# Half the tokens by fetched rows, attention and key selection in one stage, value sums kept in PSUM, and GpSimd making every second low part of the expert tiles

## The reference

```python
def memory_cross_attention(h, m, w_xq, w_xkv, w_xo):
    q = (h @ w_xq).reshape(b, s, XA_HEADS, XA_HEAD_DIM)          # 4 heads of 256
    sc = einsum('bshd,bmhd->bhsm', q, k) / sqrt(XA_HEAD_DIM)
    o = einsum('bhsm,bmhd->bshd', softmax(sc), v).reshape(b, s, D_MODEL)
    return o @ w_xo

def peer_ffn(h, w_pq, sub_keys, u_emb, v_emb):                   # 8 heads, 2 x 128 keys, 16384 experts
    q = (h @ w_pq).reshape(b, s, PEER_HEADS, 2, PEER_HALF)
    sc = einsum('bshpc,pnc->bshpn', q, sub_keys)
    top_v, top_i = top_k(sc, 16)
    cand = top_v[..., 0, :, None] + top_v[..., 1, None, :]
    best_v, best_i = top_k(cand, 16)                             # 16 experts of a token and head
    expert = i1 * 128 + i2 ; gate = softmax(best_v)
    a = einsum('bthkd,btd->bthk', u_emb[expert], h)
    return einsum('bthk,bthkd->btd', gelu(a) * gate, v_emb[expert])
```

## Time and profile before

| | us |
|---|---|
| median of 3 runs | 4000.87 (3989.51 to 4028.2) |
| the profiled execution | 3974.28 |
| its span | 3972.5 |
| first head of the selection on DVE starts | about 1712 |
| gate steps | about 2700 to 2944 |
| value groups and tail | about 2944 to 3972.5 |

### The profile page before, as it was taken

One profiled execution on the slowest core, in us unless ns is written; L12 is line 12 of the kernel. 1 busy time (PEld: TensorE's weight loads), 2 busy tenths in 40 slices (PEclk: granted clock), 3 DMA queues, 4 the chain that ended last, 5 costly groups with the idle time before them and its releaser, 6 DMA issues. The chain is left out here.

```text
span 3972.5 us, 61578 instructions
## 1 busy us (share of the span) xinstructions
PE 3687.8 (93%) x21687; PEld 3261.5 (82%) x21687; DVE 3061.8 (77%) x5229; ACT 1455.4 (37%) x2548; POOL 1648.2 (41%) x1269
## 2 busy tenths in 40 slices
PE   6999999999899999988998989998996999999996
PEld 5766676676577886778888989998996999999996
DVE  5676776777753503459999998978976999999998
ACT  3456555565652424222222222224541222222222
POOL 2433444333312120105655455552224556566552
PEclk9999999999899999999999999999998999999998
DMA  2111111111253311138888887895779999999995
GB/s 86 49 48 54 44 47 44 48 54 54 96 191 128 132 53 76 59 123 300 325 327 316 293 325 281 327 357 215 265 266 318 369 382 390 379 374 375 386 392 196
DMA packets 315022, 848.43 MB, mean 214 GB/s; under 512 B 27184, under 2 KB 122672, under 8 KB 310832
## 3 DMA queue, kind: packets, MB, share of 16 engines
q1 hardware_dynamic: 201328, 400.91, 29.4%
q0 software_dynamic: 110592, 402.70, 26.7%
q10 hardware_dynamic: 2880, 41.94, 2.7%
HBM read 726.96 MB, written 118.49 MB: 213 GB/s over the span
## 5 line engine op out<-in xcount | busy, mean ns | idle before, releaser
L1920 POOL DMA_INDIRECT join_urow<-in_u_rows,select_row_now x384 | 510.6, 1330 | 508.3 <-DVE join_rows L2221 223.0
L2672 POOL DMA_INDIRECT spread_vrow<-in_v_rows,spread_row_of x384 | 540.1, 1407 | 409.4 <-DVE spread_y L2740 301.8
L163 PE MATMUL spread_banks<-spread_ahi,spread_vhi 128*128 128x384 f32 (+1 forms) x2048 | 640.7, 313 | 55.7 <-DVE spread_acc L2730 40.3
L163 PE MATMUL select_products<-h_hi,shared_pair_hi 128*128 128x256 f32 (+2 forms) x1856 | 608.4, 328 | 71.5 <-DVE shared_raw_low L1736 66.3
L164 PE MATMUL spread_banks<-spread_alo,spread_vhi 128*128 128x384 f32 (+1 forms) x2048 | 638.2, 312 | 0.0
L165 PE MATMUL spread_banks<-spread_ahi,spread_vlo 128*128 128x384 f32 (+1 forms) x2048 | 638.0, 312 | 0.0
L164 PE MATMUL select_products<-h_lo,shared_pair_hi 128*128 128x256 f32 (+2 forms) x1856 | 603.2, 325 | 0.0
L165 PE MATMUL select_products<-h_hi,shared_raw_low 128*128 128x256 f32 (+2 forms) x1856 | 602.4, 325 | 0.0
L163 PE MATMUL shared_carry<-shared_wide_hi,shared_w_hi 128*128 128x512 f32 x1408 | 558.0, 396 | 27.7 <-DVE shared_wide_lo L591 11.2
L164 PE MATMUL shared_carry<-shared_wide_lo,shared_w_hi 128*128 128x512 f32 x1408 | 553.4, 393 | 0.0
L165 PE MATMUL shared_carry<-shared_wide_hi,shared_w_lo 128*128 128x512 f32 x1408 | 553.0, 393 | 0.0
(11 more groups left out here) (307 smaller groups left out, 6664.0 us busy)
## 6 DMA issues: line engine op xcount, KB each, us to landing
spread_vraw<-in_peer_v SPq DMA_DIRECT2D x124, 512.0 KB, 8.7
shared_raw<-in_select_pairs SPq DMA_DIRECT2D x112, 512.0 KB, 6.5
gates<-spread_stage ACTq DMA_DIRECT2D x20, 2048.0 KB, 7.3
spread_act<-gelu_u SPq DMA_DIRECT2D x128, 320.0 KB, 7.5
spread_graw<-gates SPq DMA_DIRECT2D x32, 1280.0 KB, 11.8
gelu_u<-front SPq DMA_DIRECT2D x100, 320.0 KB, 6.9
shared_w_raw<-in_w_mix SPq DMA_DIRECT2D x56, 512.0 KB, 3.6
shared_w_raw<-in_w_cross SPq DMA_DIRECT2D x32, 512.0 KB, 3.5
```

Of the source, the lines that this page charges most:

```text
L163: nc.tensor.matmul(out, whi, xhi, start=(first and i == 0), stop=False)
L1920: nc.gpsimd.indirect_dma_start(picks.slots[s][:], None, u_rows, bass.IndirectOffsetOnAxis(row_now[:, t, j:j + 1], 0)).then_inc(row_loaded[ ...
L2672: nc.gpsimd.indirect_dma_start(v_slots[s][:], None, v_rows, bass.IndirectOffsetOnAxis(row_of[:, par, t, j:j + 1], 0)).then_inc(row_loaded[ ...
```

## The change

`GT` is 4: 512 tokens, the first half, are fetched ones and the second half is dense (`PICKED` and `DENSE`). Cross attention and selection become one phase, `retrieve_phase`, with one list of tiles (`tile_order`) whose products pass through four PSUM banks in turn (`bank_order`, `Banks`), and four buffers for tiles in their raw, high and low form (`WeightTiles`). The first half's attention goes first and the second half's query projection is laid between its units. Selection runs in 16 blocks: 8 heads of the fetched half, then 8 of the dense half, each over 4 token tiles; each query tile is loaded for both halves. The 128 tiles of `peer_u` lie in blocks 2 to 15, each one product of 512 columns. The second half's output projection, residual and norm lie in blocks 0 and 1. The 512 dots are spread over blocks 1 to 15, with 7 buffers. The expert numbers are found with 16-bit integers, subtract and minimum, in place of a multiplication.

Which engine makes a low part is `maker`: GpSimd for the attention's `ask` and `give` tiles and for odd expert tiles, DVE for the rest. GpSimd's program has the lows among its fetches, in one queue:

```diff
+GT = 4
+TD = ND * P
...
+        self.maker = [int(tile[0] in ("ask", "give") or tile[0] == "expert" and tile[2] % 2) for tile in self.order]
...
+    def load(self, sync, n, src):
+        job = self.order[n - 4]
+        sync.wait_ge(self.banks.filled(job), self.banks.turn(job))
+        sync.dma_start(self.raw[n % 4], src).then_inc(self.loaded[n % 4], 16)
...
+    def split_low(self, eng, of, n):
+        eng.wait_ge(self.high_made, n + 1)
+        of.tensor_tensor(self.low[n % 4], self.raw[n % 4], self.high[n % 4].bitcast(F32), ALU.subtract
+                         ).then_inc(self.low_made[self.maker[n]], 1)
...
+    tiles += query(0) + query(1) + [("give", 1, k) for k in range(NC)] + query(2)
+    for b in range(FIRST_DENSE, BLOCKS):
+        for i, e in enumerate(experts_of(b)):
+            tiles.append(("expert", 1, e))
+            if i == QUERY_BEHIND and b + 1 < BLOCKS:
+                tiles += query(b + 1)
...
+            def experts_low(d):
+
+                for b in range(FIRST_DENSE, BLOCKS):
+                    tiles_now, dots_now = STARTS[b + 1] - STARTS[b], dots_before(b + 1) - dots_before(b)
+                    for n in range(STARTS[b], STARTS[b + 1] if b + 1 < BLOCKS else len(ORDER)):
+                        if ORDER[n][0] == "expert" and tiles.maker[n]:
+                            behind = dots_before(b) + (n - STARTS[b] - 2) * dots_now // tiles_now
+                            if min(behind, DOTS - 1) == d:
+                                tiles.split_low(pool, nc.gpsimd, n)
+
+            for d in range(DOTS):
+                fetch(d)
+                experts_low(d)
+                if d >= ROWS_SLOTS - 1 and (d - ROWS_SLOTS + 1) % 3 == 0 and (d - ROWS_SLOTS + 1) // 3 + 3 < NC:
+                    give_low((d - ROWS_SLOTS + 1) // 3 + 3)
```

The value phase has no expert tiles. Its 32 gate steps take four picks each, and the first four of them one low part of the first values. PE adds the products of all 32 groups up in eight PSUM banks, each of 512 dense tokens, so the additions on DVE go; one addition of the residual is left at the end. A group's DVE body has 16 places:

```diff
+            for q in range(NQ):
+                load_values(1, q)
...
+            sync.wait_ge(g_done, N * NB)
+            for g in range(2, NG):
+                load_tile(g, 0)
+                load_tile(g, 1)
+                load_values(g, 0)
+                load_tile(g, 2)
+                load_values(g, 1)
+                load_tile(g, 3)
+                load_gates(g)
+                load_values(g, 2)
+                load_values(g, 3)
...
+                weigh_picks(EARLY * n, EARLY * n + EARLY)
+                if n < NQ:
+                    low(0, n)
...
+                for w in range(PLACES):
+                    weigh_picks(*picks_of(g, w, PLACES))
+                    if g + 1 < NG:
+                        e, turn = divmod(w, 3)
+                        if turn == 0 and e < E:
+                            weigh(g + 1, e)
+                        if turn == 2 and e < E:
+                            split(g + 1, e)
+                    if w == 1 and g:
+                        low(g, NQ - 1)
+                    if g + 1 < NG and w in LOWS:
...
+            LOWS = (4, 8, 12)
...
+                        mm = three_pass(nc, banks[:, k], [(vhi[:, q, e, dp], vlo[:, q, e, dp], ahi[g % 2][:, e], alo[g % 2][:, e])],
+                                        first=(g == 0 and e == 0), last=(g == NG - 1 and e == E - 1))
```

More of the change, by code:

```diff
@@ new lines, in bank_order, with weighed @@
+def bank_order():
+    tiles = tile_order()
+    given, opened = tiles.index(("give", 0, 0)), tiles.index(("query", 0, 0))
+    ends = tiles.index(("query", 2, 1))
+    def weighed(half, hd):
+        return [("weigh", half, 2 * hd + c) for c in range(2)]
+    jobs = [("sum", 0, h) for h in range(2)] + tiles[:tiles.index(("ask", 1, 0))]
+    for u in range(NC):
+        if u in (3, 5, 7):
+            jobs += weighed(0, (u - 3) // 2)
+        jobs.append(("ask", 1, u))
+    jobs += weighed(0, XH - 1) + tiles[given:opened] + [("sum", 1, 0)]
+    for hd in range(XH):
+        jobs += weighed(1, hd)
+    return jobs + tiles[opened:ends] + [("sum", 1, 1)] + tiles[ends:]
@@ L1272, in cross_attention_phase @@
[L1272 to L1282, removed]
@@ L1360, in _ @@
[L1360 to L1366, removed]
+            sync.dma_start(x_in[:, NC - 1], xT[:, NC - 1]).then_inc(last_stored, 16)
+            sync.dma_start(gain[:], ffn_gain).then_inc(gain_loaded, 16)
@@ L1374, in _ @@
[L1374 to L1389, removed]
+            for n, tile in enumerate(ORDER):
+                if tile[0] == "ask" or tile[:2] == ("give", 0):
+                    tiles.split_low(pool, nc.gpsimd, n)
@@ new lines, in _, with query, scores @@
+            weigh(1, XH - 1)
+            def query(b, c):
+                half = b // PH
+                tiles.product(pe, ("query", b, c), hhi[half], hlo[half], H, (h2_low, lambda k: k + 1) if b == 0 and c == 0 else None)
+            def scores(b):
+                if b == 0:
+                    pe.wait_ge(keys_loaded, 16)
+                    pe.wait_ge(h_copied, GT)
+                else:
+                    pe.wait_ge(sc_made, 2 * b)
+                for c in range(2):
+                    tile = ("query", b, c)
+                    pe.wait_ge(banks.emptied(tile), banks.turn(tile))
+                    for t in range(ND):
+                        mm = nc.tensor.matmul(scps[:, c, t], asked[b % 2][c][:, t * P:t * P + P], keys[:, c], start=True, stop=True)
+                    mm.then_inc(scored, 1)
@@ L1575, in _, with alone @@
         @block.vector
         def _(dve):
-            def h_of(k):
+            tt, ts = nc.vector.tensor_tensor, nc.vector.tensor_single_scalar
+            def alone(sem, value):
+                dve.wait_ge(sem, value)
+                dve.sem_inc(held, 1)
+            jobs = [("sum", 0, h) for h in range(2)]
+            for job in jobs:
+                dve.wait_ge(banks.filled(job), banks.turn(job))
+            norm.start(nc, dve, [(SIDE[h], banks.at(jobs[h])) for h in range(2)], lambda h: sum_read[h])
```

2197 lines of the change are left out of this document (930 added, 1267 removed).

## The result

The changed kernel takes 4738.59 us (median of 4 runs, 4734.8 to 4750.42), the kernel before 3995.19 us on the same chip: a ratio of 1.1859, 95% interval 1.177 to 1.1947. Slower was forecast, at 4230 us and at most 4370; the loss is three times as large. The profiled execution took 4734.98 us.

What follows compares the result with a forecast made beforehand. DVE, held by GpSimd's lows, was taken to bound blocks and gate steps. Earlier start -64, blocks and phase change +285, gate steps +76, value sums -62 gave +235 us, hence 4230 us, range 4040 to 4370.

Steps and rivals of the forecast that it cites:

- Up to the first keys: Projections and attention before selection: first block's selection starts at 1648 instead of 1712, a gain of 64 us.
- The blocks: Selection blocks with expert tiles: 14 at 80 us, bounded by DVE, with PE's 62 and DMA's 69 us under it.
- The hold of a GpSimd low: In the blocks: each low part made on GpSimd costs DVE 2.1 us, 9.6 us a block.
- half of before's: DVE's idle time in a block: half of the earlier selection's 5.4 us per head, 2.7 us.
- rival (4): Blocks: lows waiting in GpSimd's queue hold up gathers and starve DVE's dots, 4 to 8 us each; 4490 us; chance 0.14.
- for the pair that meets the next: Earlier gate steps: a GpSimd low costs DVE 2.2 us for the operation pair that meets the next low.
- Gate steps: After the blocks: 32 steps of 9.7 us with four picks each, 320 us against 244 before.
- Value groups: Value sums: 28.5 us a group, 18.9 up to the gates' load issue plus its landing, against 29.1 before.
- The landing: Value groups: the gates' load lands 9.6 us after issue, within bounds of 6.3 and 11.6.
- (2): PE was the bound: blocks at 62 us, groups at 27.5, total 3950 us, not slower; chance 0.06.
- (3): Lows on GpSimd are free for DVE: blocks of 69 us, groups at 27.5, total 4045 us; chance 0.14.
- The start of the value stage and the tail: Value stage besides 30 groups: 22 us first gates, 16 second load, 23 first body, 15.5 last, 35 tail.

Runs made afterwards that it cites:

- run 7: Changed kernel with all expert lows on DVE and two buffers for the gates: 4051.78 us, ratio 1.0163 to the kernel before.
- run 8: run 7 with the dots and picks of the fourth fetched token tile on 8 of 1024 columns, all transfers kept: 3945.21 us, ratio 0.9896.
- run 6: Changed kernel with GpSimd's lows 7 fetches later in its queue and two buffers for the gates: 4100.9 us, ratio 1.0287.
- run 1: Changed kernel with GpSimd's lows of the odd expert tiles 7 fetches later in its queue: 4406.98 us, ratio 1.1008.
- run 2: Changed kernel with all 128 expert lows on DVE, none on GpSimd: 4356.81 us, ratio 1.0883.
- run 5: Changed kernel without 499 of the 512 transfers of peer_v rows, later picks reusing the first 13 rows: 4490.5 us, ratio 1.1264.

## Why the prediction was wrong

The direction was right, for the reason given: DVE's dots and picks bound the blocks and gate steps (runs 7 and 8), and the redesign loses 1.6% with both waits gone. Even there the sum was too high: with both waits gone and the lows on GpSimd (run 6) it loses 111 us, where 235 were summed; blocks of 76.6 us for 80 and groups of 26.9 for 28.5 are some 100 of the difference. The size was not right: the span was forecast at some 4207 us and was 4733, 526 more, 271 from block 2 to the gate steps and 255 in the value stage.

- *Up to the first keys:* forecast 1648, measured 1661. Block 0: 25, measured 22 (first searches at 1660.8 and 1682.6). Block 1: 108, measured 105. Right to a few us.
- *The blocks, 80 us each: the step that failed.* DVE's work was near: 77.2 us a block were summed without idle time, 937.14 us busy in 13 blocks are 72.1, and run 1, where next to nothing waits, has 75.0 of 76.6. The hold of a GpSimd low was right too, 2.1 us forecast and 2.2 measured. What failed is the idle time, "half of before's", 2.7 us; it measured 29.1 (378 in 13 blocks), 28.4 of it DVE's wait for fetched rows. So rival (4) was true, which had the mechanism and got a chance of 0.14. I reckoned how long a low *may* wait (4 us) and did not ask how long it *would*, though the code says it: the low of tile n stands behind the fetch of the dot that belongs to tile n - 2, the fetches run 7 dots ahead, with 34.1 dots over 11.14 tiles another 2.3 tiles, and the high part of n exists only after tile n - 3 is emptied. So the low comes up over a tile too early every time. A row for the wait stood there too: 177.8 us for 24 lows in the gate steps are 7.4 us each, above the 4 that were allowed. GpSimd waited 7.8 us a low (326 us in 42, from 1785 to 2720), DVE 389.4 / 64 = 6.1 us, in the middle of the "4 to 8 us" of the rival. Moving it by those 7 fetches took it all away (run 1). The hold then is a cost of its own, shown by run 2. (The 2.2 us "for the pair that meets the next" are not in the earlier trace rows; in the trace such a pair took 4.56 us from 2916.36, against 2.35.)
- *Gate steps:* 320, measured 314, 9.8 a step for 9.7. Right.
- *Value groups, 28.5 us each: mechanism right, a term mis-sized.* The load of the gates is issued behind the last split and DVE waits at every top of a group, 32 times. The landing was taken as 9.6 us "since the load goes out when only one or two others are under way", within bounds of 6.3 and 11.6. It is 15.4, outside, because of the gathers (run 5: 7.4 without them), and the same picks that precede the wait let a row of them go. That is 5.8 of the 8.4 us a group that were missing; 1.7 are a wait for ScalarE's high part of the values (46.1 us over some 27 groups), and 0.9 are left unexplained.
- *Rivals (2) and (3)* are out: in the blocks PE is at 71%, and a low on GpSimd costs DVE 2.2 us.
- The start of the value stage and the tail, all but 30 groups: 111.5 us forecast, 115 measured.

## What to carry to other kernels

An instruction that is put into a queue between others needs its own due time: when its input exists, against when the queue reaches it. Count both in the same units, fetches or tiles, before asking how much slack the queue has. A load with one buffer is paid at every turn with its landing, less the work that stands behind its issue (here DVE waits for 11.3 of the 15.4 us), and that landing is not the median of the kernel before but what the queue holds at the moment of issue; a second buffer took it off the path here, an earlier issue did not. Work given to GpSimd is not free for VectorE when VectorE's operations have two inputs: here it cost 2.2 us to save 1.2.

## What the runs showed that was not expected

- Lengthening a landing can be harmless and shortening its way useless: 18.0 us with two buffers cost nothing, and an issue some 3 us earlier brought 3.0 us more of landing (18.4).
- The granted clock of PE fell with the waits, from 0.96 and 0.99 in the long stages before to 0.84 in blocks and groups and 0.58 in the gate steps, where PE is busy for 110 of 314 us; with both waits gone it is back at 0.95 in the blocks (run 7). None of these three stages was bound by PE, so no price can be put on it.
